# Norms of the stick-breaking heads: squares summed as plain float32 in two 64-column products, one logarithm for q and k

## What is computed

```python
def head_rms_norm(x, g):
    xf = x.astype(jnp.float32)
    y = xf * lax.rsqrt(jnp.mean(xf * xf, axis=-1, keepdims=True) + EPS)
    return y * g.astype(jnp.float32)
...
qn = head_rms_norm(q_b.reshape(B, S, H_B, HD_B), sb_q_norm_g[l])
kn = head_rms_norm(k_b.reshape(B, S, H_B, HD_B), sb_k_norm_g[l])
y_b = stick_breaking(qn, kn, v_b...)   # z = qn.kn / sqrt(128), sigmoids, suffix products, times v
```

## Time and profile before

| | |
|---|---|
| median of 3 runs | 1235.97 us (1235.95 to 1236.13) |
| the profiled execution's own time | 1235.73 us |
| its span | 1233.5 us |
| TensorE busy | 1219.5 us, 99% of the span |
| VectorE busy | 784.0 us, 64% |
| ScalarE busy | 637.1 us, 52% |
| GpSimd busy | 72.1 us, 6% |
| share of TensorE on the chain that ended last | 87% |
| share of VectorE on that chain | 9% |

### The profile page before, as it was taken

The page is one execution under the profiler, slowest core; times in us unless marked ns, Lnnn a source line. Parts: engine busy times, 40 slices in busy tenths (PEclk is TensorE's granted clock), DMA queues, the critical chain, the costliest instruction groups (busy, mean ns, idle before and its releaser), DMA issues.

```text
span 1233.5 us, 15642 instructions
## 1 busy us (share of the span) xinstructions
PE 1219.5 (99%) x5856; PEld 994.6 (81%) x5856; DVE 784.0 (64%) x1226; ACT 637.1 (52%) x926; POOL 72.1 (6%) x148
## 2 busy tenths in 40 slices
PE   8999999999999999999999999999999999999998
PEld 7888888888888888888888888878867777777887
DVE  7735644683654466468476483797579989656671
ACT  7645544654554462554443462546466555566720
POOL 2101110210111021000000000000000000000000
PEclk9999999999999999999999999999999999999999
DMA  5421322332132236214216123124213333635621
GB/s 212 144 79 35 111 68 77 102 100 86 35 111 69 77 103 224 103 35 165 74 52 219 37 102 137 35 86 170 74 65 119 110 130 111 228 115 179 239 69 69
DMA packets 25607, 134.22 MB, mean 109 GB/s; under 512 B 3337, under 2 KB 3513, under 8 KB 12753
## 3 DMA queue, kind: packets, MB, share of 16 engines
q1 hardware_dynamic: 16224, 107.14, 25.0%
q0 software_dynamic: 4720, 16.90, 3.9%
q10 hardware_dynamic: 4608, 9.44, 2.0%
HBM read 121.92 MB, written 11.55 MB: 108 GB/s over the span
## 4 chain that ended last, share of the span: by engine, by line
PE 87%; DVE 9%; issue 2%; ACT 1%; DMA 0%; ACTq 0%; DVEq 0%
PE proj L313 63%; PE proj L1852 5%; PE pm L1852 2%; PE pa L1852 2%; PE pm L1753 1%; DVE w_lo L286 1%; PE pa L1764 1%; PE pa L2046 1%; PE pa L1725 1%; PE pm L1735 1%; DVE idx L1470 1%; PE proj L1774 1%; PE pa L1774 1%; PE pa L2026 1%; PE pa L1744 1%
## 5 line engine op out<-in xcount | busy, mean ns | idle before, releaser
L313 PE MATMUL proj<-h_hi,w_hi 128*128 128x512 f32 (+1 forms) x840 | 328.8, 391 | 0.6 <-ACT acts L753 0.6
L313 PE MATMUL proj<-h_hi,w_lo 128*128 128x512 f32 (+1 forms) x840 | 323.9, 386 | 0.0
L313 PE MATMUL proj<-h_lo,w_hi 128*128 128x512 f32 (+1 forms) x840 | 323.6, 385 | 0.0
L286 DVE TENSOR_TENSOR w_lo<-w_raw,w_hi 128x2048 fp32r<-128x2048 f32 x84 | 191.5, 2288 | 58.4 <-ACT w_hi L280 58.1
L280 ACT ACTIVATE w_hi<-w_raw 128x2048 fp32r<-128x2048 f32 x84 | 159.6, 1913 | 69.1 <-PE proj L1852 48.1
L313 PEld LDWEIGHTS proj<-h_hi,w_hi 128*128 128x128 f32 x840 | 157.9, 188 | 36.0 <-issue 5.0
L313 PEld LDWEIGHTS proj<-h_hi,w_lo 128*128 128x128 f32 x840 | 157.8, 188 | 32.0
L313 PEld LDWEIGHTS proj<-h_lo,w_hi 128*128 128x128 f32 x840 | 158.0, 188 | 31.4 <-issue 1.0
L313 PE MATMUL proj<-w_hi,h_hi 128*128 128x512 f32 (+1 forms) x288 | 112.6, 391 | 0.3 <-issue 0.3
L313 PE MATMUL proj<-w_lo,h_hi 128*128 128x512 f32 (+1 forms) x288 | 111.7, 388 | 0.0
L313 PE MATMUL proj<-w_hi,h_lo 128*128 128x512 f32 (+1 forms) x288 | 111.5, 387 | 0.0
(11 more groups left out here) (463 smaller groups left out, 2121.6 us busy)
## 6 DMA issues: line engine op xcount, KB each, us to landing
w_raw<-in_wall SPq DMA_DIRECT2D x92, 1024.0 KB, 5.0
b<-in_wall SPq DMA_DIRECT2D x8, 1024.0 KB, 6.1
gates<-gate_st ACTq DMA_DIRECT2D x24, 256.0 KB, 2.0
m_all<-gates POOLq DMA_DIRECT2D x2, 1280.0 KB, 6.9
x_res<-in_x ACTq DMA_DIRECT2D x4, 512.0 KB, 5.0
bc<-gate_rows POOLq DMA_DIRECT2D x8, 256.0 KB, 3.4
x_res<-in_x POOLq DMA_DIRECT2D x4, 512.0 KB, 4.2
x<-x_res POOLq DMA_DIRECT2D x1, 2048.0 KB, 8.9
```

The source lines that it names most:

```text
L286: nc.vector.tensor_tensor(w_lo[:, slot, 4 * half:4 * half + 4, :], w_raw[:, half], w_hi[:, slot, 4 * half:4 * half + 4, :], ALU.subtract)\
L313: mm = nc.tensor.matmul(proj[:, bank, 0:cols] if tokens else proj[:, bank, toks], lhsT, rhs, start=(k == 0 and q == 0), stop=(k == kts - 1 ...
```

## The change

`qk_tile` writes the float32 square first and signals `sq_made`, then the copy, which frees the PSUM bank; the square rounded to fp32r, and VectorE's low part of it, are gone. `square_sums` waits for both squares once and makes two plain float32 matmuls with 64 columns of ones: q's sums go to partitions 0 to 63 of one bank of `pa`, k's to partitions 64 to 127. One logarithm covers both and is written to `sq_k`; then four exponentials of 64 partitions each spread the result: the lower half to both halves of `sq_q`, the upper half to both halves of `sq_k`. Between the second and the third stands a wait, since the third overwrites what the first two read.

```diff
--- before.py
+++ after.py
@@ -320,6 +320,7 @@
 
 
         NORM_ORDER = (1, 0, *range(2, KT))
+        HALF = (slice(0, P // 2), slice(P // 2, P))
 
         def norm_bank(k):
             if k < 2:
@@ -611,20 +612,21 @@
                 a.wait_ge(S["tile_made"], n + 1)
                 if heads is not None:
                     a.wait_ge(S["z_made"], heads)
-                a.activation(raw[:, :], proj[:, j], ACT.Copy)
-                a.activation(sq_hi[:, j], proj[:, j], ACT.Square)
-                a.activation(sq[:, :], proj[:, j], ACT.Square).then_inc(S["tile_free"], 1)
+                a.activation(sq[:, :], proj[:, j], ACT.Square).then_inc(S["sq_made"], 1)
+                a.activation(raw[:, :], proj[:, j], ACT.Copy).then_inc(S["tile_free"], 1)
 
             def conv_tile(h, n):
                 a.wait_ge(S["tile_made"], n + 1)
                 a.wait_ge(S["head_done"], h + 1)
                 a.activation(qk_pad[:, 3:3 + SEQ], proj[:, 0], ACT.Copy).then_inc(S["tile_free"], 1)
-                for j, sq in enumerate((sq_q, sq_k)):
-                    a.wait_ge(S["ssq_made"], 2 * h + j + 1)
-                    a.activation(sq[:, :], pa[:, 512 * j:512 * (j + 1)], ACT.Ln, bias=eps[:, 0:1], scale=1.0 / HD_B)\
-                        .then_inc(S["rms_ln"], 1)
-                    a.wait_ge(S["rms_ln"], 2 * h + j + 1)
-                    a.activation(sq[:, :], sq[:, :], ACT.Exp, scale=-0.5).then_inc(S["rms_b"], 1)
+                a.wait_ge(S["ssq_made"], h + 1)
+                a.activation(sq_k[:, :], pa[:, 0:SEQ], ACT.Ln, bias=eps[:, 0:1], scale=1.0 / HD_B).then_inc(S["rms_ln"], 1)
+                a.wait_ge(S["rms_ln"], h + 1)
+                for j, r in enumerate((sq_q, sq_k)):
+                    if j:
+                        a.wait_ge(S["rms_b"], 4 * h + 2)
+                    for rows in HALF:
+                        a.activation(r[rows, :], sq_k[HALF[j], :], ACT.Exp, scale=-0.5).then_inc(S["rms_b"], 1)
                 for j, raw in enumerate((q_b, k_b)):
                     a.wait_ge(S["qk_normed"], 2 * h + j + 1)
                     a.activation(sq_hi[:, j], raw[:, :], ACT.Copy).then_inc(S["qk_hi"], 1)
@@ -1099,10 +1101,6 @@
             v.tensor_tensor(g_m[:, :], g_F[:, :], g_G[:, :], ALU.add).then_inc(S["rows_m"], 1)
             v.tensor_scalar(g_out[:, 0, :], g_G[:, :], -1.0, None, ALU.mult).then_inc(S["rows_ready"], 1)
 
-            def square_low(n, j):
-                v.wait_ge(S["tile_free"], n + 1)
-                v.tensor_tensor(sq_lo[:, j], (sq_q, sq_k)[j][:, :], sq_hi[:, j], ALU.subtract).then_inc(S["sq_lo"], 1)
-
             def head_start(h):
                 v.wait_ge(S["head_done"], h + 1)
                 v.tensor_copy(par[:, :], hp[:, bass.ds(h, 1), :].rearrange("p a n -> p (a n)")).then_inc(S["par_head"], 1)
@@ -1122,7 +1120,7 @@
 
             def qk_norms(h):
                 for j, (raw, r) in enumerate(((q_b, sq_q), (k_b, sq_k))):
-                    v.wait_ge(S["rms_b"], 2 * h + j + 1)
+                    v.wait_ge(S["rms_b"], 4 * h + 2 * j + 2)
                     v.scalar_tensor_tensor(raw[:, :], raw[:, :], sbg[:, j:j + 1], r[:, :], ALU.mult, ALU.mult)\
                         .then_inc(S["qk_normed"], 1)
                 for j, raw in enumerate((q_b, k_b)):
@@ -1201,14 +1199,12 @@
                     .then_inc(S["head_done"], 1)
 
             split_lo(G_HEADS + 1, 0, 0)
-            square_low(T_HEADS, 0)
             split_lo(G_HEADS + 1, 0, 1)
             v.wait_ge(S["par_landed"], 80)
             v.wait_ge(S["a_turned"], 1)
             for i, dst in enumerate((a_col, e_col)):
                 v.tensor_copy(dst[:, :, :], pm[:, TB * HEADS * i:TB * HEADS * (i + 1)].rearrange("p (t h) -> p t h", h=HEADS))\
                     .then_inc(S["a_col"], 1)
-            square_low(T_HEADS + 1, 1)
             v.wait_ge(S["a_col"], 2)
 
             def pair(p, more=True):
@@ -1232,8 +1228,6 @@
 
                 h = 2 * p + 1
                 head_start(h)
-                for j in range(2):
-                    square_low(n + 10 + j, j)
                 qk_norms(h)
                 conv_taps(h, n + QKA[1])
                 split_lo(g + 4, 1, 0)
@@ -1245,12 +1239,9 @@
                 if more:
                     split_lo(g + 5, 0, 0)
                     v.wait_ge(S["a_done"], h + 1)
-                    square_low(n + NEXT, 0)
                 token_norm(h)
                 gated_y(h, n + O_A[1], n + G_A[1])
-                if more:
-                    square_low(n + NEXT + 1, 1)
-                else:
+                if not more:
                     split_lo(g + 5, 0, 0)
                 head_end(h, n + G_B[1])
                 split_lo(g + 5, 0, 1)
@@ -1712,11 +1703,10 @@
 
             def square_sums(h):
                 t_.wait_ge(S["pv_read"], h + 1)
-                for j in range(2):
-                    t_.wait_ge(S["sq_lo"], 2 * h + j + 1)
-                    t_.matmul(pa[:, 512 * j:512 * (j + 1)], ones_r[:, :], sq_hi[:, j], start=True, stop=False)
-                    t_.matmul(pa[:, 512 * j:512 * (j + 1)], ones_r[:, :], sq_lo[:, j], start=False, stop=True)\
-                        .then_inc(S["ssq_made"], 1)
+                t_.wait_ge(S["sq_made"], 2 * h + 2)
+                for j, sq in enumerate((sq_q, sq_k)):
+                    mm = t_.matmul(pa[HALF[j], 0:SEQ], ones[:, 0:P // 2], sq[:, :], start=True, stop=True)
+                mm.then_inc(S["ssq_made"], 1)
 
             def stick_scores(h):
                 t_.wait_ge(S["qk_lo"], 2 * h + 2)
```

## The result

| | before | changed |
|---|---|---|
| median | 1235.95 us (1235.85 to 1236.13, 7 runs) | 1240.18 us (1239.87 to 1240.41, 7 runs) |
| ratio to before | | 1.0034, 95% interval 1.0024 to 1.0044 |
| profiled execution, own time | 1235.73 us | 1240.38 us |
| span | 1233.5 us | 1238.2 us |

The change makes the kernel 4.2 us slower. The forecast was 3.3 us, 1239.3, with its own range from 1237.8 to 1240.9. (The profiled execution of each kernel lies 0.2 us from its median.)

A forecast was written before the change was run, and what follows sets the result against it. TensorE, busy throughout the heads, bounds the kernel; +2.7 us for the squares and +0.6 for the wait on normed k make +3.3 on 1235.73, so 1239.0, or 1239.3 for the median; range 1237.2 to 1242.4.

The forecast's parts named there:

- The bound: In the heads TensorE is always busy, so its additions reach the end and time saved on ScalarE or VectorE counts nothing.
- The two products on TensorE: Squares' sums: 0.86 for the side-by-side pair, 0.15 ahead, 0.23 behind, 1.24 against 0.90 us; +0.34 a head, +2.7 in all.
- The serial rival: The squares' two products run one after the other: 2.11 us, +1.21 a head, 1246.3 us in all; chance 5%.
- The rule quoted beside this rival: Trainium skill: a weight load overlaps matmuls in flight only if its row group differs; two column tiles share rows.
- The third rival: Not slower: 512-column last product hides the loss behind the squares, leaving 0.25 us a head, +2.0, 1238.0 us; chance 12%.
- The chain behind the sums: Norm of k 1.06 us later against 0.59 margin; TensorE's scores wait 0 to 0.20, taken 0.08 a head, +0.6 us.
- The norm's rival: Half-width exponentials 0.66 apart, or writing other partitions costs: normed k 0.3 to 0.6 us later, 1241.7 to 1244.1; chance 10%.

The follow-up runs named there:

- e1: The changed kernel with the stick scores issued after the first three matmuls of the following projection tile; 1238.38 us, ratio 1.0020 to the kernel before.
- e5: The changed kernel with both 64-column float32 products into partitions 0 to 63, logarithm and two exponentials separately for q and k; 1245.54 us, ratio 1.0079.
- e3: The kernel before with its four fp32r products 64 columns wide, all into partitions 0 to 63, and 64-partition logarithms and exponentials; 1240.90 us, ratio 1.0040.
- e7: The changed kernel with the pair of products of the squares made twice, to the same place; 1247.33 us, ratio 1.0093 to the kernel before.
- e9: The changed kernel with all four exponentials from and to partitions 0 to 63, of four free tiles; 1238.48 us, ratio 1.0021 to the kernel before.
- e2: The changed kernel with two float32 products 128 columns wide, into two banks, and the earlier kernel's logarithms and exponentials; 1242.80 us, ratio 1.0056.
- e6: The changed kernel with each exponential reading the same half of the partitions that it writes; 1240.09 us, ratio 1.0035 to the kernel before.
- e4: The kernel before without the squares' low part: one rounded square, one full-width fp32r product each for q and k; 1232.16 us, ratio 0.9970.

## Why the prediction was right, and where it was off

**The bound.** Right. TensorE had no idle time in the heads, so all of its additions reached the end, and the 10.5 us that left VectorE bought nothing. ScalarE's came back as exponentials, which the working had not set against them; that by itself changed nothing either.

**The two products on TensorE, +0.34 us a head.** Right in each term: 1.01 for the pair and 0.23 behind it, both read off line 2046 before the change ran. e1 isolates this part at 2.5 us for eight heads. The serial rival is excluded: the pair's products start together and take 1.01, and e5 shows what the same two cost one after the other, 1.86. The rule quoted beside this rival in the prediction does not hold for these two halves: all four loads start between 102.17 and 102.23, while products of the same rows are under way. The third rival, that a long last product hides the loss behind, is excluded by the tile's 5.67. What I said of the cause was broader than what holds: "a change of the tiling mode" is not any product of 64 columns, as e3 shows. The section Key Properties of "TensorEngine Tiling (Array Packing)" of the Trainium skill states the drain for a change of mode; e5 and e7 agree, once per switch and 0.14 to 0.15 ahead and 0.22 to 0.23 behind, and e3 is a product of 64 columns without it.

**The chain behind the sums, +0.08 us a head.** The mechanism was right and the size was not: the wait measured 0.20 us, and this is the term that makes 4.2 of 3.3. The working had the load of the scores 0.13 us late. It was 0.31 late: TensorE's own shift puts it at 102.24 + 5.96 + 0.34 = 108.54, and it came at 108.85. Three amounts make that up: the 0.13; 0.13 more of the norm of k (1.19 instead of 1.06); and 0.05 from the end of VectorE's step to the load, which I had left out. The 0.13 of the norm is itself two misreadings that partly cancel. The step "from an exponential's start to the next activation 0.54" was read off full-width activations, and the half-width ones of this kernel start 0.66 apart, twice: 0.24 too little (e9 gives the 0.24 of both pairs back, 0.27 with all that hangs on it, and with them the wait). And the 0.16 from q's products to the first logarithm was no delay of the sums: the logarithm stood behind ScalarE's copy, and the real step from the sums is 0.04 (0.03 in e2, from 103.22 to 103.25), so 0.12 too much. That is why the logarithm came 0.44 us later than before (1.05 behind the start of the squares, 0.61 before) and not 0.56. That the forecast came as near as it did is partly luck: with only the logarithm read rightly, the working would have had the load 0.01 us late, no wait at all, and 1238.7. Of the 0.31, 0.11 is the load's lead, which was spare, as the working supposed of a part of it. e1 removes the wait and nothing else, and gets 1.8 us back; 8 x 0.20 = 1.6. The term ended at its upper bound of 0.20, and the time at 1240.2 near the upper end of the forecast's own range.

**The norm's rival** named this overlap, "0.66 instead of 0.54", as one of its two causes, and that cause holds. Its price of 0.3 us and above was too high: of the three steps between four exponentials one has a wait and was counted at 0.66 already, so only two lose 0.12 each, 0.24 us, and 0.12 of that had been counted by the late logarithm. So this rival's cause is at work inside the forecast, at a smaller size than it was given. Its second cause, writing to other partitions than those read, is excluded by e6.

What the upper half does to ScalarE is shown only so far: in e9 all four exponentials use the lower half and start 0.53 to 0.54 apart, while in the changed kernel and in e6 each pair has one that uses the upper half, and the activation behind an exponential of the upper half also starts 0.66 behind it. No run has two upper-half exponentials of different tiles in a row, and whether reading or writing the upper half decides, no run told apart. Activations of all 128 partitions, which use the upper half too, start 0.54 apart.

## What to carry to other kernels

Two products side by side must save more than the switch into and out of their tiling costs, here 0.38 us. One pair against four fp32r matmuls does not: 0.86 against 0.90 is all that it has to set against the switch. A pair against the same two plain float32 products in a row does, and a stretch like line 2046's still more, since it pays the switch once. Before a step is put between a producer and its consumer, count the consumer's margin in the trace (0.59 us here), then add the hops between engines, look what each engine was doing just ahead of a step whose start you read (the copy ahead of the logarithm), and read each spacing from instructions of the same shape and the same partitions, for a shift that outgrows the margin lands on the bound engine, here but for 0.11 us. Where the bound engine is full, look for what it can leave out (e4), and not for work to take off engines that wait.

## What was not expected of the hardware

- A 64-column product switches the tiling only as plain float32. Four fp32r products with 64 columns between full ones start 0.22 to 0.24 us apart like their neighbours (e3); two float32 ones pay 0.14 and 0.22 us even when both use the lower half (e5).
- The switch is paid once for a stretch: a second pair adds 0.86 us to 1.01 (e7). In the trace it shows as weight loads that lose their lead of 0.22 us over their products.
- Two exponentials of 64 partitions start 0.66 us apart if one of them uses partitions 64 to 127 (e6), and 0.53 to 0.54 apart if both stay in 0 to 63 (e9, which also writes to two tiles); reading one half and writing the other makes no difference. They last 0.61 to 0.63 us, as at full width (0.63).
